# An encoder trunk on one core: the first stage cut into token halves, and the fourth block emptied earlier

## The reference, cut to what matters

```python
h = jnp.concatenate([meta, x], axis=1)
xn = rmsnorm(h, norm_mix[i])              # h / sqrt(mean(h^2) + eps) * g
proj = xn @ m_w_in                        # q, k, v, output gate, and 16 gate columns
q, k = proj[..., :M_QK_W], proj[..., M_QK_W:2 * M_QK_W]
gpre = proj[..., 2 * M_QK_W + 2 * M_V_W:]
ig, lf = gates[0::2], jax.nn.log_sigmoid(gates[1::2])   # cumulative sums and maxima over tokens follow
h_f = mlstm_cell(q, k, v, ig[0], lf[0])   # per head: weights exp(...) * (q k^T), times v
```

## Time and profile before

| what | us |
|---|---|
| median of three runs | 1982.94 |
| profiled execution, whole time | 1983.51 |
| its span, first to last instruction | 1981.7 |
| TensorE busy | 1934.0 (98% of the span) |
| VectorE busy | 1137.5 (57%) |
| GpSimd busy | 1090.7 (55%) |
| ScalarE busy | 720.4 (36%) |

### The profile page before, as it was taken

One profiled execution on the slowest core, in us unless ns is written; L12 is line 12 of the kernel. 1 busy time (PEld: TensorE's weight loads), 2 busy tenths in 40 slices (PEclk: granted clock), 3 DMA queues, 4 the chain that ended last, 5 costly groups with the idle time before them and its releaser, 6 DMA issues.

```text
span 1981.7 us, 30261 instructions
## 1 busy us (share of the span) xinstructions
PE 1934.0 (98%) x11129; PEld 1805.8 (91%) x11129; DVE 1137.5 (57%) x1912; ACT 720.4 (36%) x1430; POOL 1090.7 (55%) x1503
## 2 busy tenths in 40 slices
PE   8999999999999999999999999999989999999998
PEld 7898988899999999999978888888878998998997
DVE  6756464777365265266566666666685562562651
ACT  4333332445143142143224444445452340430431
POOL 4523323358597596596632222222467894884973
PEclk9999999999999999999999999999999999999999
DMA  4111101212221221222211111101211222222213
GB/s 157 43 33 33 48 27 43 68 56 59 69 81 54 65 79 56 71 66 70 67 43 33 33 32 32 32 26 38 60 43 54 85 65 64 76 70 59 80 55 95
DMA packets 214920, 114.90 MB, mean 58 GB/s; under 512 B 7011, under 2 KB 213510, under 8 KB 214550
## 3 DMA queue, kind: packets, MB, share of 16 engines
q1 hardware_dynamic: 212816, 112.62, 19.4%
q10 hardware_dynamic: 1990, 0.76, 0.2%
HBM read 108.57 MB, written 4.78 MB: 57 GB/s over the span
## 4 chain that ended last, share of the span: by engine, by line
PE 85%; DVE 6%; POOL 4%; ACT 2%; DMA 2%; issue 1%; SPq 0%; DVEq 0%; ACTq 0%; POOLq 0%
PE ps L620 44%; PE ps L671 27%; PE ps L818 3%; PE ps L979 2%; PE ps L947 2%; POOL wl L552 2%; PE ps L798 1%; POOL wxl L552 1%; PE ps L969 1%; DMA raw<-in_ffn_w_in_dram 1%; PE ps L881 1%; PE ps L751 1%; PE ps L827 0%; DMA wk<-in_x_sample_dram 0%; DVE mx L1721 0%
## 5 line engine op out<-in xcount | busy, mean ns | idle before, releaser
L541 POOL CAST wh<-raw 128x256 fp32r<-128x256 f32 x428 | 165.1, 425 | 754.5 <-PE ps L620 719.8
L671 PE MATMUL ps<-sx,wh 128*128 128x400 f32 (+1 forms) x1408 | 367.3, 342 | 8.9 <-POOL wl L552 6.4
L552 POOL TENSOR_TENSOR wl<-raw,wh 128x256 fp32r<-128x256 f32 x352 | 319.7, 936 | 88.6 <-ACT wh L1905 87.9
L545 POOL TENSOR_TENSOR wl<-raw,wh 128x256 fp32r<-128x256 f32 x428 | 331.7, 804 | 10.3
L671 PE MATMUL ps<-sx,wxh 128*128 128x400 f32 (+1 forms) x1056 | 276.9, 343 | 9.1 <-ACT u L1912 8.1
L671 PEld LDWEIGHTS ps<-sx,wh 128*128 128x128 f32 x1408 | 258.4, 189 | 10.0 <-issue 6.6
L671 PE MATMUL ps<-sx,wl 128*128 128x400 f32 (+1 forms) x704 | 240.5, 342 | 0.0
L1905 ACT ACTIVATE wh<-raw 128x512 fp32r<-128x512 f32 x176 | 106.6, 627 | 363.7 <-PE ps L620 241.1
L552 POOL TENSOR_TENSOR wxl<-raw,wxh 128x256 fp32r<-128x256 f32 x220 | 223.5, 1041 | 12.7 <-ACT wxh L1905 12.7
L620 PE MATMUL ps<-xh,wh 128*128 128x400 f32 (+2 forms) x768 | 221.1, 366 | 0.0
L620 PE MATMUL ps<-xl,wh 128*128 128x400 f32 (+2 forms) x768 | 212.4, 352 | 0.0
(11 more groups left out here) (265 smaller groups left out, 3334.3 us busy)
## 6 DMA issues: line engine op xcount, KB each, us to landing
raw<-in_ffn_w_in_dram SPq DMA_DIRECT2D x154, 256.0 KB, 3.0
raw<-in_ffn_w_out_dram SPq DMA_DIRECT2D x48, 384.0 KB, 3.4
raw<-in_m_w_in_dram SPq DMA_DIRECT2D x24, 512.0 KB, 3.7
raw<-in_d_w_in_dram SPq DMA_DIRECT2D x24, 512.0 KB, 3.8
rawx<-in_ffn_w_in_dram SPq DMA_DIRECT2D x22, 256.0 KB, 3.1
raw<-in_m_w_out_dram SPq DMA_DIRECT2D x8, 512.0 KB, 4.1
raw<-in_ffn_w_out_dram SPq DMA_DIRECT2D x16, 256.0 KB, 2.7
wk<-in_x_prompt_dram SPq DMA_DIRECT2D x4, 512.0 KB, 5.7
```

The source lines that it names most:

```text
L541: ins = pool.tensor_copy(wh[:, slot, c], raw[:, slot, c])
L545: ins = pool.tensor_tensor(wl[:, slot, c], raw[:, slot, c], wh[:, slot, c].bitcast(F32), ALU.subtract)
L552: ins = pool.tensor_tensor(slot_of(j, 1)[:, c], factor(g, j)[:, c], slot_of(j, 0)[:, c].bitcast(F32), ALU.subtract)
L671: mm = pe.matmul(product_bank(g, j, layer), slot_of(j, low_w)[:, k * P:(k + 1) * P], sx[layer][:, k * NPROD + j, low_x, :], start=(j in OP ...
```

## The change: what it does

**First stage.** The tokens are handled in two halves of 400. The first half is the first sequence's meta tokens and x tiles 0 to 2. ScalarE and VectorE make `xh`, squares, `xl` and sums for the first half for all k, and then for the second half; four new semaphores (`half_xh`, `half_xl`, `half_sq`, `half_summed`) count the first half, the old ones the second. Squares go through two buffers in turn. TensorE turns tiles 0 and 1, the meta tokens, the parameters and tile 2, makes gates and block 0 of the first half, and turns tiles 3, 4 and 5 in between, after k = 0, 2 and 4. Then it makes the second half. Tiles go to bank pairs 3 and 1. The copies into `h` are: VectorE tile 0, ScalarE tile 1, half of tile 2 each, ScalarE tile 3, VectorE tile 4, half of tile 5 each. SP issues block 0's weights after tile 0, instead of after tile 3. GpSimd's wait for `xl_ready` 7 now means the seventh fold of the second half. The last `sum_squares` wait needs both counts.

**Fourth block.** In head 0 VectorE empties block 3 before the diagonals, not after them.

```diff
+X_PAIR = (3, 1)
...
                 if r == 0:
                     sp.dma_start(wkf[0:META, XT * D:(XT + 1) * D], meta_tokens).then_inc(meta_in, 16)
-                elif r == 3:
                     first_weights(0)
...
+            def gates(k, half):
+                pe.wait_ge((half_xl, xl_ready)[half], k + 1)
+                for q, (w, x) in enumerate(((gwh, xh), (gwh, xl), (gwl, xh))):
+                    mm = pe.matmul(ps[:, 4 + half, 0:HT], w[:, k, :], x[:, k, half * HT:(half + 1) * HT],
+                                   start=(k + q == 0), stop=(k == KT - 1 and q == 2), skip_group_check=True)
+                return mm
...
             for k in range(KT):
+                gates(k, 0)
+                run_block(MIX0, 0, 0, tokens="first half", k0=k, k1=k + 1)
+                if k in (0, 2, 4):
+                    turn_x(3 + k // 2)
+            for k in range(KT):
+                mm = gates(k, 1)
                 if k == KT - 1:
                     mm.then_inc(gates_done, 1)
                     sum_squares(1)
-                run_block(MIX0, 0, 0, k0=k, k1=k + 1)
+                run_block(MIX0, 0, 0, tokens="second half", k0=k, k1=k + 1)
...
+            def fold_half(k, half):
+
+                a, b = half * HT, (half + 1) * HT
+                ve.wait_ge((half_xh, xh_ready)[half], k + 1)
+                ve.scalar_tensor_tensor(xl[:, k, a:b], h[:, k, a:b], par[:, MIXN + k:MIXN + k + 1], xh[:, k, a:b].bitcast(F32),
+                                        ALU.mult, ALU.subtract).then_inc((half_xl, xl_ready)[half], 1)
...
             for k in range(KT):
+                fold_half(k, 0)
+                if k == 2:
+                    keep_x(4, slice(0, KT))
+                elif k == 4:
+                    keep_x(5, slice(KP, KT))
...
                 ve.wait_ge(mrep_ready, hd * 2 + 2)
+                if first:
+                    evacuate(n + 3, 1, wk[:, 7, :])
                 for j in OF_SEQ[0]:
                     diagonals(j)
...
-                evacuate(n + 3, 1, wk[:, 7, :])
+                if not first:
+                    evacuate(n + 3, 1, wk[:, 7, :])
...
             for k in range(KT):
+                fold_half(k, 0)
+                if k == 1:
+                    keep_x(3, slice(0, KT))
+                elif k == 4:
+                    keep_x(5, slice(0, KP))
```

More of the change, by code:

```diff
@@ L614, in run_block @@
                          "inner": [(flat(p)[:, a:b], t, t + b - a) for a, b, t in SEGS],
-                         "packed": [(flat(p)[:, a:b], a, b) for a, b, t in SEGS]}[tokens]
+                         "packed": [(flat(p)[:, a:b], a, b) for a, b, t in SEGS],
+                         "first half": [(ps[:, 2 * p, 0:HT], 0, HT)],
+                         "second half": [(ps[:, 2 * p + 1, 0:HT], HT, T)]}[tokens]
                 for k in range(k0, k1 or k_tiles):
@@ L624, in run_block @@
                             del small[:1]
-                    if k == k_tiles - 1:
+                    if k == k_tiles - 1 and tokens != "first half":
                         mm.then_inc(block_done, 1)
@@ L634, in sum_squares @@
                          [(flat(3)[:, a:b], t, t + b - a) for a, b, t in SEGS])
+                if count == 1:
+                    pe.wait_ge(half_summed, KT)
                 for out, a, b in parts:
-                    mm = pe.matmul(out, ones[:, :], src[:, a:b], start=True, stop=True)
+                    of = wk[:, 1, :] if count == 1 and a == 0 else src
+                    mm = pe.matmul(out, ones[:, :], of[:, a:b], start=True, stop=True)
                 mm.then_inc(norm_sum, 1)
@@ L1471, in keep_x @@
                 ve.tensor_copy(h[:, tiles, t0:t0 + P],
[L1472 to L1480, removed]
+                               flat(X_PAIR[r % 2]).rearrange("p (k c) -> p k c", k=KT)[:, tiles, :]).then_inc(x_kept_even, 1)
+            def fold_half(k, half):
[3 more added lines that the diff above has]
+                                        ALU.mult, ALU.subtract).then_inc((half_xl, xl_ready)[half], 1)
+                done = (half_summed, sq_summed)[half]
+                ve.wait_ge((half_sq, sq_ready)[half], k + 1)
+                squares, total = wk[:, 7 * half, (k % 2) * HT:(k % 2 + 1) * HT], wk[:, (1, 6)[half], a:b]
+                if k == 0:
+                    ve.tensor_copy(total, squares).then_inc(done, 1)
+                else:
+                    ve.wait_ge(done, k)
+                    ve.tensor_tensor(total, total, squares, ALU.add).then_inc(done, 1)
+            keep_x(0, slice(0, KT))
+            ve.wait_ge(meta_turned, 1)
+            for s in range(2):
+                ve.tensor_copy(h[:, :, START[s]:START[s] + META],
+                               ps[:, 4, 0:KT * META].rearrange("p (k c) -> p k c", k=KT)).then_inc(h_ready, 1)
             ve.wait_ge(par_turned, 1)
             ve.tensor_copy(par[:, :], ps[:, 5, 0:NPAR]).then_inc(par_ready, 1)
-            keep_x(XT - 1, slice(KP, KT))
-            ve.wait_ge(x_kept_even, XT // 2 + 1)
-            ve.wait_ge(x_kept_odd, XT // 2)
+            keep_x(2, slice(KP, KT))
+            ve.wait_ge(x_kept_even, 2)
+            ve.wait_ge(x_kept_odd, 2)
             ve.wait_ge(h_ready, 2)
@@ L1488, in _ @@
             for k in range(KT):
-                fold(k, k, par[:, MIXN + k:MIXN + k + 1])
-                add_first_square(k)
+                fold_half(k, 0)
[3 more added lines that the diff above has]
+                    keep_x(5, slice(KP, KT))
+            ve.wait_ge(x_kept_even, 4)
+            ve.wait_ge(x_kept_odd, 4)
+            for k in range(KT):
+                fold_half(k, 1)
             v(ve.memset(wk[:, 4, :], 0.0))
```

79 lines of the change are left out of this document (41 added, 38 removed).

## The result

The changed kernel took 1990.69 us (median of five, 1989.0 to 1991.62), the kernel before 1981.58 us beside it (1979.69 to 1983.38). The ratio is 1.0044, 95% interval 1.003 to 1.0059: slower by 8.7 us, 5.9 to 11.7. Forecast were +5.4 us and 1988.3, range 1984.3 to 1992.5. The direction and the range held; the size was 3 us short.

What follows compares the result with a forecast made beforehand. TensorE was taken as the bound: nothing to multiply until 18.64 us, then not seen waiting until 73. First stage +6.2 and fourth block -0.8 gave +5.4 us: 1983.5 to 1988.9, as a median 1988.3; range 1984.3 to 1992.5.

Steps and rivals of the forecast that it cites:

- part 2: First half on TensorE: late tiles' transposes and copies queue between products and folds; waits 0.6, 2.0, 2.1 us; +4.8 us.
- part 1: Start of the first half on TensorE: first product at about 15.7 us instead of 18.64, 2.9 us gained.
- The parameters: Rival at the first half's start: parameters land at 14.1 us, total 1991.1; chance 0.10 for late parameters or tiles together.
- The clock: TensorE in the first half: clock at 0.50 for about 5.6 us from the first product at 15 to 16.5 us.
- the clock falls in the new pauses: Rival, TensorE's pauses at tiles 4 and 5 or the scores: clock falls, total 1992.1 or 1991; chance 0.13.
- part 3: GpSimd's block 1 weights: low parts done at 46.4 us, TensorE ready at 45.0, so block 1 starts 6.2 us later.
- released by GpSimd's low part, not by TensorE: Sign at block 1: it starts at 46 to 47 us, waiting for GpSimd's weights rather than for TensorE.
- part 4: After block 1: VectorE's chain moves with TensorE, and no slack gives the 6.2 us back.
- part 5: Fourth block in head 0: evacuation ahead of the diagonals gains 0.8 of 1.9 us; bounds 0 to 1.1.
- The wait ahead of the scores: TensorE in head 0, before the scores: wait grows from 1.28 to about 2.4 us.
- The sum: Whole kernel: +6.2 - 0.8 = +5.4 us, 1988.9 for the profiled execution, 1988.3 as a median.

Runs made afterwards that it cites:

- the first trace: Profiled execution of the changed kernel in its first run, no further edit against it; 1989.65 us, where the run's median was 1990.69 us.
- the second: Trace of the changed kernel run once more with no edit; median 1990.58 us against 1982.11 for the kernel before, ratio 1.0044.
- the trace with two falls: Trace of the kernel before with only the first stage's change, without the fourth block's; median 1992.88 us against 1982.11, ratio 1.0051.
- all tiles ahead: Changed kernel, still in halves, with all six tiles turned and copied ahead of the first fold; 1984.5 us against 1982.11 for the kernel before, ratio 1.0011.

## Why the prediction was right, and what was mis-sized

*The queue's order (part 2)* was right and is shown. Waits of 0.6, 2.0 and 2.1 us were forecast, 1.21, 1.86 and 1.87 came. (The first depends on how long the lower level lasts: 0.37 and 0.87 in two other traces of the stage.) Turning each tile one place earlier on TensorE's queue removes them and with them the whole loss.

*The first product (part 1)* was forecast at 15.7 and came at 16.66. The mis-sized terms are the arrival of tile 1 and the turning: tile 1 began at 9.22 instead of 8.8, and tile 1, the meta tokens with the parameters, and tile 2 took 1.90, 1.22 and 1.97 us where the sum has 1.7, 1.0 and 1.7. I priced the moved weights as 1.36 us of transfer. They also part the turning in two: before, it ran without a break from 5.90 and was past the low pace when it came to tile 3 at 11.58 (1.09 us); here TensorE stood still for 1.40 us and was still at the low pace for tile 2 at 12.34. In the medians that edit alone costs 2.4 us. "Full clock" for the turning was read off the clock column, against the durations beside it; the sum did use the low pace there. The parameters, which I feared for, were no cause: they were there by 12.1.

*The clock.* Forecast was the lower level for 5.6 us from the first product on. In the first trace it ended some 3 us after the first product, in the second after 5.5, as forecast. The rival "the clock falls in the new pauses" came true in addition, though in the first trace shorter than priced: 3.4 us at the lower level, which cost 1.5. I had argued against it from pauses of 1.81 and 1.28 us that left the clock up. Pauses of 1.86 and 1.87 did not, so those rows did not carry the argument. That the time at block 1 came out near is in part luck: the first product was 1.0 us late, the early rise of the clock gave most of this back (TensorE took up k = 5 at 31.84, my 31.6), and the fall then put 1.5 on, so that TensorE was 1.9 later than my 45.0 and block 1 0.5 later than my 46.4, which I had from GpSimd. In other traces of the same stage the clock cost more.

*GpSimd (part 3)* was ready at 46.2, forecast 46.4, by casts of 2.27 and low parts of 2.80. (The terms given in the forecast add up to 46.1; 0.3 us of it is not named.) GpSimd did not set block 1, because TensorE was later than I had it; it did where the clock was kept up, by 0.79 us. So the sign "released by GpSimd's low part, not by TensorE" was not met in the changed kernel.

*No slack later (part 4)* held: the shift at 120 us is that of 1299 us within 0.4, and that of the end within 1.2.

*The fourth block (part 5)* gave 1.7 us, not 0.8. My bounds of 0 to 1.1 were too narrow, since I took the diagonals' 3.50 us as their own length; moved, they took 2.39. The wait ahead of the scores came to 1.49 us, not 2.4.

*The sum*: +5.4 forecast, about +8.7 measured. The traces show +6.7 at block 1, +4.9 at the scores and +6.1 at the end, so against its own trace the sum was good to 0.7 us, and some 3 us of the median's shift stand in no trace of the changed kernel. The profiled execution of before lay 1.9 us above the median of its runs and the two of the changed kernel 1.0 and 2.3 below theirs. The clock is one candidate (the sum of squares comes 1.9 us later in the trace with two falls); the cause of the 3 us stays open.

## What to carry to other kernels

When work is cut so that it starts while inputs still come in, look at each queue: the copy of the next piece stands in the same queue as the work on the current one, and if its input is made only just before, the engine in front waits for the round trip. Make the input one step earlier than the copy asks for it; that was worth 9 us here by the medians, 6 to 7 in the traces of the first 50 us, for no other edit. And look twice before putting a large transfer ahead of a stream of inputs that keeps TensorE busy: it cost 2.4 us in the kernel before and 4.2 with all tiles ahead, and nothing that could be told in the changed kernel and in the one with the transposes a step earlier.

## What the runs showed of the hardware

- TensorE's level can be read from the pace where the clock column does not tell it: 0.33 us per product of 400 columns at the lower, 0.18 at the upper, while the column said 1.00 in both stretches (16.6 to 19.2 and 36.8 to 45.0 us).
- After pauses of 1.86 and 1.87 us, 5 us apart, the clock was down for 3.4 us in the first trace, which cost 1.5 us; it fell in all four traces with these pauses, in two of them behind both. With the pauses filled by products it did not fall there.
- Where VectorE's ten diagonals (2.39 us) and GpSimd's four subtractions (2.8 us) meet, one pays 1.1 to 1.7 us; moving the evacuation ahead of the diagonals changed which one. One subtraction of 0.74 us then took 2.38, while nearly the whole row of diagonals ran at its own pace.
- Executions of the same stage differ by the time that the clock is down (sum of squares at 45.0, 45.5 and 46.9 in three traces), so one trace each can't tell two kernels that lie 1 to 2 us apart.
